# Five pairs of weight buffers moved by 0, 8, 16, 24 and 32 bytes inside on-chip memory

## What is computed

```python
# first block
p = h @ w_in                       # 1024 x 9232: q, k, v, z, a, beta, scb, scc, scx, gate a, gate b
y_a = o.reshape(b, s, V_W) @ w_gdn_proj
y_b = (gb * conv(gc * xin)) @ w_sc_out
mix = (gate_a * y_a + gate_b * y_b) @ w_o
x = x + g2 * ((silu(gu[..., :D_FF]) * gu[..., D_FF:]) @ w_ffn_out)    # gu = h @ w_ffn_in
# second block
qkv = y @ w_qkv ; h = h + attention(q, k, v) @ w_o
h = h + (silu(gate) * val) @ w_down                                   # gate, val = conv(y @ w_up)
return rms_norm_2(h, final_norm)
```

## Time and profile before

| | us |
|---|---|
| median of 3 runs | 913.32 |
| lowest and highest | 912.99, 917.46 |
| the profiled execution's own time | 921.88 |
| its span, first to last instruction | 920.1 |

### The profile page before, as it was taken

How to read it: one execution, slowest core, us unless ns; L and a number is a source line. 1 busy time by engine, 2 the same in 40 slices (tenths; PEclk the granted TensorE clock), 3 DMA queues, 4 the chain that set the end, 5 groups by cost and what they waited for, 6 DMA issues and landing times.

```text
span 920.1 us, 18632 instructions
## 1 busy us (share of the span) xinstructions
PE 893.8 (97%) x8020; PEld 850.1 (92%) x8020; DVE 667.6 (73%) x1132; ACT 505.1 (55%) x814; POOL 65.8 (7%) x83
## 2 busy tenths in 40 slices
PE   5998999999999999999999999999999999999997
PEld 2798998999898999999999999999899999999997
DVE  4878767566978677677798775588665688778652
ACT  2489667454354627555354444466665576666442
POOL 0100201021001001020000000120000200000011
PEclk9999999999999999999999999999999999999999
DMA  8754233333767665465988889526331455555631
GB/s 335 279 191 162 102 129 104 128 138 109 259 232 247 209 229 179 165 217 179 288 326 295 287 287 255 218 96 226 138 138 53 177 184 192 190 192 178 223 126 46
DMA packets 27681, 177.31 MB, mean 193 GB/s; under 512 B 2864, under 2 KB 5680, under 8 KB 7504
## 3 DMA queue, kind: packets, MB, share of 16 engines
q1 hardware_dynamic: 27600, 176.13, 54.7%
HBM read 174.29 MB, written 1.84 MB: 191 GB/s over the span
## 4 chain that ended last, share of the span: by engine, by line
PE 82%; DVE 8%; ACT 6%; DMA 2%; issue 1%; DVEq 0%; SPq 0%; ACTq 0%
PE ps L1093 46%; PE ps L1099 22%; PE ps L1091 2%; DVE wl L1841 2%; DVE acc L1740 1%; ACT wh L1454 1%; PE ps L1138 1%; PE ps L1146 1%; PE ps L1232 1%; PE ps L1149 1%; PE ps L1097 1%; DMA raw<-in_ada_dram 1%; PE ps L1252 1%; PE ps L1303 1%; DMA raw<-in_w_sc_dram 1%
## 5 line engine op out<-in xcount | busy, mean ns | idle before, releaser
L1093 PE MATMUL ps<-HH,wh 128*128 128x256 f32 x1480 | 374.1, 288 | 0.7 <-DVE wl L1841 0.2
L1841 DVE TENSOR_TENSOR wl<-raw,wh 128x1024 fp32r<-128x1024 f32 x265 | 320.2, 1228 | 73.4 <-ACT wh L1454 72.8
L1093 PE MATMUL ps<-HH,wl 128*128 128x256 f32 x1480 | 361.0, 279 | 0.0
L1454 ACT ACTIVATE wh<-raw 128x1024 fp32r<-128x1024 f32 x265 | 273.8, 1043 | 142.5 <-PE ps L1099 112.9
L1093 PEld LDWEIGHTS ps<-HH,wh 128*128 128x128 f32 x1480 | 280.4, 189 | 9.8 <-issue 4.3
L1093 PEld LDWEIGHTS ps<-HH,wl 128*128 128x128 f32 x1480 | 279.8, 189 | 1.9 <-issue 1.9
L1099 PE MATMUL ps<-HL,wh 128*128 128x256 f32 x1480 | 229.1, 279 | 0.3 <-DVE HL L1786 0.3
L1099 PEld LDWEIGHTS ps<-HL,wh 128*128 128x128 f32 x1480 | 197.1, 189 | 0.6 <-DVE HL L1786 0.5
L1093 PE MATMUL ps<-FH,wh 128*128 128x256 f32 x352 | 85.9, 278 | 0.0
L1093 PE MATMUL ps<-FH,wl 128*128 128x256 f32 x352 | 85.9, 278 | 0.0
L1740 DVE SCALAR_TENSOR_TENSOR acc<-raw,silc,acc 128x512 f32<-128x512 f32 x101 | 76.3, 756 | 8.0 <-DMA raw<-in_ada_dram 4.9
(11 more groups left out here) (269 smaller groups left out, 1080.9 us busy)
## 6 DMA issues: line engine op xcount, KB each, us to landing
raw<-in_ada_dram SPq DMA_DIRECT2D x32, 1024.0 KB, 5.2
raw<-in_w_fi_dram SPq DMA_DIRECT2D x22, 1024.0 KB, 4.9
raw<-in_w_up_dram SPq DMA_DIRECT2D x22, 1024.0 KB, 4.8
raw<-in_w_rest_dram SPq DMA_DIRECT2D x20, 1024.0 KB, 4.8
raw<-in_w_in_dram SPq DMA_DIRECT2D x16, 1024.0 KB, 4.8
raw<-in_w_qkv_dram SPq DMA_DIRECT2D x12, 1024.0 KB, 4.8
raw<-in_w_o_dram SPq DMA_DIRECT2D x8, 1024.0 KB, 4.8
raw<-in_w_fo_dram SPq DMA_DIRECT2D x8, 1024.0 KB, 5.0
```

Of the source, the lines that this page charges most:

```text
L1093: e.matmul(o, w[:, k, 128 * t:128 * t + 128], x_hi[:, k0 + k, :], start=first and n + k == 0, **MM)
L1454: e.activation(whl[u % HALF][0][:, 0:n], raw[i % RAW][:, c:c + n], ACT.Copy).then_inc(*a_hi.up(u))
L1841: e.tensor_tensor(wl[:, 0:n], raw[i % RAW][:, c:c + n], wh[:, 0:n].bitcast(F32), ALU.subtract).then_inc(*v_lo.up(u))
```

## The change

The five pairs of buffers become views of one tensor `W`. Pair i begins at element 2050 i, that is at byte 8200 i; the low part follows 4096 bytes behind the high part. Since 8192 is a multiple of 512, the pairs lie 128, 136, 144, 152 and 160 bytes past a multiple of 512 (before: 128 all). `W` is 8 floats longer than the ten buffers were, so `X` moves by 32 bytes, to 160; `home_x` is 8 floats shorter, so `HH` and all that follows keep their places, and so does `raw`. No instruction is added, removed or moved, and no wait.

```diff
     raw = [sb(f"raw{i}", [128, 2048]) for i in range(RAW)]
-    whl = [(sb(f"wh{i}", [128, 1024], F32R), sb(f"wl{i}", [128, 1024], F32R)) for i in range(HALF)]
+
+    W = sb("W", [128, 2048 * HALF + 8], F32R)
+    whl = [tuple(W[:, 2050 * i + 1024 * n:2050 * i + 1024 * n + 1024] for n in range(2)) for i in range(HALF)]
     X = sb("X", [128, 8, T])
 
-    sb("home_x", [128, 112])
+    sb("home_x", [128, 104])
     HH = sb("HH", [128, 8, T], F32R)
```

## The result

The changed kernel is slower: 925.10 us median of 4 runs (923.56 to 926.05) against 913.15 us (911.15 to 917.46, 4 runs) for the kernel before, a ratio of 1.0123 with a 95% interval of 1.0084 to 1.0161. Its profiled execution took 924.93 us, with a span of 923.1, only 3.0 us more than that of the profiled execution before. This gap between the two comparisons is part of the answer: the profiled execution before, at 921.88 us, held the slow pace through the whole last stretch. That its plain runs, 4.4 to 10.7 us shorter, held it less is inferred, since they have no trace.

What follows compares the result with a forecast made beforehand. TensorE's distance between product matmuls was taken as the bound. Cutting slow stretches short saves 9.2 us: 921.88 to 912.7 profiled, in the same ratio 904.2 for the 913.32 median, shaded to 905; range 897 to 922.

Steps and rivals of the forecast that it cites:

- The sign in the earlier trace: Weight loads: median 188 ns 64 bytes from moving rows, 192 where both begin at the same place modulo 512.
- the 111 ns of the warming ones: Warming matmuls on TensorE: best pace found for a full weight load with as much streaming, taken as the floor.
- the mechanism of the forecast: On TensorE, a distance step at each pair change disturbs the slow pace, which mostly settles into the quick one.
- its only term: TensorE's weight loads: slow stretches end at the next pair change, 2041 matmuls x 4.5 ns = 9.2 us saved.
- the prediction's own bound: All product matmuls on TensorE at the quick pace: 15.3 us saved, 898.
- a third pace that depends on the distance: Sign on TensorE: a pace neither 113.3 nor 117.8 would say the distance in bytes sets the pace itself.
- rival 3: TensorE's quick stretches gain too, as a distance of 72 to 96 bytes suits the reads: 898 to 884; chance 0.05.
- the 9.2 us of the profiled execution: Saving on TensorE from nine listed slow stretches cut short, subtracted from the profiled 921.88 us to give 912.7.
- its three chances: Of the whole kernel's time: faster 0.40, same 0.32, slower 0.28; a change under 0.5%, 4.6 us, hardly told from none.
- Rival 1: The step does nothing on TensorE, the two paces come from inside it and its queue: 913; chance 0.32.
- Rival 2: TensorE loads slower in pairs 1 and 3, 8 bytes off a multiple of 16: 918.4 or 924.6; chance 0.27.
- the bound of all slow: All product matmuls on TensorE at the slow pace: 12.8 us lost, 926.

Runs made afterwards that it cites:

- the two kernels with one odd pair: Pairs 0 to 3 at distance 64, pair 4 at 96 (918.52 us, 1.0038) or at 8 (915.15 us, 1.0000), ratios to the kernel before.
- the eight kernels with slow distances in all pairs or in all but one: All pairs at 136, the changed kernel with rows 32 bytes higher, and six maps with another distance per pair: ratios 1.0159 to 1.0256 to the kernel before.

## Why the prediction was wrong

**What it had right.** The bound and the reading of it: TensorE's distance between starts, two paces of 113.3 and 117.8 ns, neither from the clock nor from the load of DMA or other engines. That places in memory matter to it. The sign in the earlier trace rows was a real one: with distances 0 and 256, the loads of product matmuls have a median of 192 ns too (worked out from the trace). But it is no measure of the pace: at 72 the median is 188 as at 64, and the pace 118.3 ns. Zero for instructions, for `X`, and for ScalarE and VectorE at odd starts: the low parts still take 1238 ns. That product matmuls would not reach the 111 ns of the warming ones: no distance came under 113.3 ns. And the mechanism of the forecast exists: in the changed kernel no long slow stretch stands at distance 64. From 752 us to the end pair 0 is quick in every turn, as it is in the two kernels with one odd pair; the unit before that, taken in pieces from 735.5 us, was not (117.7 ns).

**The step that failed** is the first of its only term: "Within one unit nothing changes in kind: the distance in bytes between load and moving rows is constant." I took the distance to matter only through its steps, and priced the five distances alike. The distance itself sets the pace. Where the forecast put all pairs at 113.3 ns after a reset, the five have 113.6, 118.6, 118.6, 113.6 and 117.5, on average 3.1 ns over the quick pace. Over 6264 matmuls that is an estimate of 19.4 us above a kernel that is quick throughout; by the prediction's own bound that one takes 921.88 - 15.3 = 906.6 us, which makes 926.0 us, and 925.1 was measured.

That the two agree so well is in part luck, as the two profiled executions show when their product matmuls are matched one by one. Up to 357 us the changed kernel gains 0.8 us, although its mean distance between starts there is 117.3 ns against 115.6: other waits take up the difference. From 357 us to the last stretch it loses 5.8 us. In the last stretch, 1575 distances, it gains 2.1 us (183.4 for 185.5), where the forecast had 7. From 357 us on, all distances together lie 10.7 us over 113.3 ns each in the kernel before and 14.9 us in the changed one. So the pace is paid for in the last 560 us, and a kernel that is quick there would take about 921.88 - 10.7 = 911 us rather than 906.6; the shortest run of the kernel before in any series took 910.5. The prediction did write down the sign by which this would show, a third pace that depends on the distance, but gave it no rival, price or chance of its own, except on the quick side (rival 3).

**A second error** made the gain look larger. I carried the 9.2 us of the profiled execution over to the median run nearly whole, and shaded the 904.2 up by only 0.8 us, to 905. Later series of the kernel before ran from 910.5 to 923.3 us with medians of 914.4 and 914.1: the likely reading, though plain runs have no trace, is that the slow pace is dealt in each run and that the profiled one at 921.88 had drawn much of it. A median run lies 3 us above the 911 that the trace gives for a quick one, and 4 above the shortest run; the slow stretches that I counted cannot give it 9. A smaller slip: by the prediction's own terms its three chances come to 0.39, 0.31 and 0.30, where it gives 0.40, 0.32 and 0.28.

**The rivals.** Rival 1 (nothing happens) fell: the eight kernels with slow distances in all pairs or in all but one are 1.6 to 2.6% slower. Rival 2 came near in time, 924.6 us at its dear end, and had the right sign, but its mechanism is wrong: pairs 1 and 3 were to be slow for lying 8 bytes off a multiple of 16, and pair 3 is quick, pairs 2 and 4 are slow on multiples of 16, and all five at 152 cost nothing. The range ended at 922 because it stopped between the two forms of that rival; the bound of all slow, 926, had been worked out and left outside.

**The rule cited.** The Trainium skill, "SBUF — State Buffer", section "Who interferes with whom", has TensorE's two reads independent, and the prediction took from it that no address can matter. The runs here do not agree with that: with the same instructions and waits and the full clock, moving only the weights of all pairs by 8 bytes against the rows takes away the quick pace of 113.3 ns and leaves 118.3. Why certain distances are quick is not shown; that the two reads of TensorE contend for memory is one reading, but no run looked inside. Nor is it known why the pace at 64, 76, 88 and 320 has two values, and what in a change of work or of distance decides between them.

## What to carry to other kernels

Where a kernel is bound, as this one, by the distance from one pair of weight load and matmul to the next, the place of the weights against the moving rows is a parameter worth up to 2.6% here: measure the pace from start to start for each buffer, not the mean over a ring, because buffers that take turns can hide a slow one. Give all buffers of a ring the same tested distance; a stagger moves most of them off a good place. And before pricing a gain from one profile, see whether that execution lies at the median of the runs: a pace that can differ from one execution of the same kernel to the next can be worth more than the edit.

## What was not expected of the hardware

- The pace of a load and matmul pair (128 x 128 weights, 256 moving columns, 32 bits) depends on the bytes between the two operands: 113.3 ns at 64 and 88, 114.9 at 76, 116 to 121 ns at all others tried except 320 (like 64), 4 bytes away from a quick place already 118.4 to 120.0.
- Distances 0 and 256 ran alike (119.8 and 119.7 ns), 64 and 320 too, 0 and 128 did not.
- At 64 and 88 there are two paces each, and a pace once taken can stand for hundreds of matmuls, even through steps between these two distances (467 matmuls counted in 54.5 us).
- The pace of a unit depends on the pace before it as well: distance 96, entered from 64, ran at 117.2 ns after a slow unit and at 120.1 after a quick one.
- A weight load that starts 8 bytes off a multiple of 16 cost nothing by itself (all pairs at 152: 1.0002).
